# Splitting the low parts of the normalised rows between GpSimd and VectorE, ahead of a mixture-of-experts gather

## The reference

```python
xn = rms_norm(h, ffn_norm_g)                     # rows of 1024, scaled by 1/rms, times a gain
group_prob = softmax(xn @ w_rg + b_rg)           # 4 groups, the best one is taken
sel = (xn @ w_re + b_re)[the group's 8 experts]  # the best two of them, by softmax
for e in range(32):
    hid = silu(xn @ w_gate[e]) * (xn @ w_up[e])
    out = out + (hid * cw[..., e:e+1]) @ w_down[e]
```

## Time and profile before

| | |
|---|---|
| median of 3 runs | 946.12 us (946.02 to 948.24) |
| the profiled execution | 947.29 us |
| its span, first to last instruction | 945.3 us |
| TensorE busy | 932.9 us, 99% |
| VectorE busy | 532.9 us, 56% |
| ScalarE busy | 469.9 us, 50% |
| GpSimd busy | 4.4 us, 13 instructions |
| granted TensorE clock, mean | 0.997 of full speed |

### The profile page before, as it was taken

How to read it: one execution, slowest core, us unless ns; L and a number is a source line. 1 busy time by engine, 2 the same in 40 slices (tenths; PEclk the granted TensorE clock), 3 DMA queues, 4 the chain that set the end, 5 groups by cost and what they waited for, 6 DMA issues and landing times.

```text
span 945.3 us, 14062 instructions
## 1 busy us (share of the span) xinstructions
PE 932.9 (99%) x5793; PEld 759.7 (80%) x5793; DVE 532.9 (56%) x835; ACT 469.9 (50%) x728; POOL 4.4 (0%) x13
## 2 busy tenths in 40 slices
PE   9999999999999999999999999999999999999996
PEld 8989887888889999999889888889876565666553
DVE  5888996775766555655686875676454212122213
ACT  5588846857454544444566756445452131313113
POOL 1000000000000000000000000000000000000000
PEclk9999999999999999999999999999999999999998
DMA  9945565525555555554645735466758999999993
GB/s 322 315 138 176 180 223 178 164 104 179 178 187 191 179 179 179 178 184 152 210 152 180 231 130 164 148 244 245 272 187 321 406 409 408 409 409 409 409 409 123
DMA packets 89861, 223.55 MB, mean 236 GB/s; under 512 B 9161, under 2 KB 14018, under 8 KB 89794
## 3 DMA queue, kind: packets, MB, share of 16 engines
q1 hardware_dynamic: 87488, 219.62, 64.8%
q10 hardware_dynamic: 2306, 2.99, 0.9%
HBM read 221.54 MB, written 1.05 MB: 235 GB/s over the span
## 4 chain that ended last, share of the span: by engine, by line
PE 95%; DMA 3%; DVE 1%; ACT 0%; issue 0%; ACTq 0%
PE pb L494 22%; PE pb L496 21%; PE pb L495 21%; PE pb L2505 11%; PE pb L2528 5%; PE pb L2545 3%; DMA my<-in_w_exp_down 2%; PE pb L2479 2%; PE pb L584 2%; PE pb L664 1%; PE pb L652 1%; PE pb L751 1%; PE pb L635 1%; PE pb L602 1%; PE pb L728 1%; PE pb L558 1%
## 5 line engine op out<-in xcount | busy, mean ns | idle before, releaser
L1567 DVE TENSOR_TENSOR wl<-raw,wh 128x2048 fp32r<-128x2048 f32 (+3 forms) x112 | 246.3, 2207 | 96.3 <-ACT wh L1017 96.0
L1017 ACT ACTIVATE wh<-raw 128x2048 fp32r<-128x2048 f32 (+3 forms) x112 | 206.7, 1853 | 110.3 <-PE pb L496 102.3
L494 PE MATMUL pb<-wh,th 128*128 128x512 f32 (+2 forms) x620 | 245.8, 396 | 0.0
L496 PE MATMUL pb<-wh,tl 128*128 128x512 f32 (+2 forms) x620 | 239.0, 385 | 0.0
L495 PE MATMUL pb<-wl,th 128*128 128x512 f32 (+2 forms) x620 | 238.6, 385 | 0.0
L494 PE MATMUL pb<-th,wh 128*128 128x256 f32 x528 | 152.7, 289 | 0.0
L495 PE MATMUL pb<-tl,wh 128*128 128x256 f32 x528 | 149.3, 283 | 0.0
L496 PE MATMUL pb<-th,wl 128*128 128x256 f32 x528 | 149.3, 283 | 0.0
L496 PEld LDWEIGHTS pb<-wh,tl 128*128 128x128 f32 x620 | 116.4, 188 | 23.3
L494 PEld LDWEIGHTS pb<-wh,th 128*128 128x128 f32 x620 | 116.5, 188 | 23.0 <-issue 2.2
L495 PEld LDWEIGHTS pb<-wl,th 128*128 128x128 f32 x620 | 116.7, 188 | 20.7
(11 more groups left out here) (424 smaller groups left out, 1116.8 us busy)
## 6 DMA issues: line engine op xcount, KB each, us to landing
raw<-in_w_in SPq DMA_DIRECT2D x31, 1024.0 KB, 5.5
raw<-in_w_up SPq DMA_DIRECT2D x16, 1024.0 KB, 5.6
raw<-in_w_down SPq DMA_DIRECT2D x16, 1024.0 KB, 6.1
raw<-in_w_exp_up SPq DMA_DIRECT2D x10, 1024.0 KB, 15.7
raw<-in_w_xkv SPq DMA_DIRECT2D x8, 1024.0 KB, 5.1
raw<-in_w_exp_down SPq DMA_DIRECT2D x8, 1024.0 KB, 17.5
raw<-in_w_exp_gate SPq DMA_DIRECT2D x6, 1024.0 KB, 18.2
S<-in_w_exp_down SPq DMA_DIRECT2D x6, 1024.0 KB, 17.1
```

The source lines that it names most:

```text
L494: PE.matmul(o, lh, rh, start=start, stop=False, skip_group_check=True)
L496: return PE.matmul(o, ll, rh, start=False, stop=stop, skip_group_check=True)
L1017: ACTE.activation(hi_of(i), raw_of(i), ACT.Copy).then_inc(S["hi"], 1)
L1567: DVE.tensor_tensor(lo_of(i), raw_of(i), hi_of(i).bitcast(F), ALU.subtract).then_inc(S["lo"], 1)
```

## The change

The low parts of the first token tile are no longer made by VectorE but by GpSimd, in two instructions of 128x1024: the view of `X` times the root into a new tile `XT0`, and `XT0` minus the high part into XNL. GpSimd waits for the root (`rs`) before the first, and for ScalarE's first high half (`xn_hi`) before the second. VectorE makes the four low parts of the second tile. TensorE's low pairs wait for both.

```diff
@@ pool_main
             POOL.memset(SEL0[:, :].bitcast(F).rearrange("p (a n) -> p a n", n=64)[:, :, CAP:64], 0.0).then_inc(S["zero"], 1)
+            hi, lo = [x[:, 0] for x in XN4]
+            POOL.wait_ge(S["used"], ROUTER + 1)
+            POOL.wait_ge(*scaled("ffn"))
+            POOL.tensor_scalar(XT0, by_chunks[:, 0], rs_of["ffn"][:, 0:1], None, ALU.mult).then_inc(S["xn_scaled"], 1)
+            POOL.wait_ge(S["xn_hi"], 1)
+            POOL.wait_ge(S["xn_scaled"], 1)
+            POOL.tensor_tensor(lo, XT0, hi.bitcast(F), ALU.subtract).then_inc(S["xn_lo0"], 1)
@@ dve_route
             for r in range(4):
-                for t in range(2):
-                    low(t, r)
+                low(1, r)
@@ pe_gather
                 if q == 0 and 1 in parts:
-                    PE.wait_ge(S["xn_lo"], 2 + 2 * (k // 2))
+                    PE.wait_ge(S["xn_lo0"], 1)
+                    PE.wait_ge(S["xn_lo"], 1 + k // 2)
@@ build
         XN = [sbe("XNH", 2048, R, normed), sbe("XNL", 2048, R, normed)]
+        XT0 = sbe("XT0", 1024, F, normed)[:, :].rearrange("p (k q) -> p k q", k=8)
```

More of the change, by code:

```diff
@@ L153 @@
      "t2_mm", "t2", "xs_mm", "xmax", "xexp", "xprob", "xt_mm", "xt", "xv_mm", "xo_hi", "xo_lo", "xs_scaled", "logits",
-     "route_e", "mask_d", "xo_first", "rank_mm", "root", "sums", "flag", "rank", "weights", "xn_hi", "xn_lo",
+     "route_e", "mask_d", "xo_first", "rank_mm", "root", "sums", "flag", "rank", "weights", "xn_hi", "xn_lo", "xn_scaled", "xn_lo0",
      "sel", "cs_w", "ch_mm", "ch", "g_mm", "g_x", "rise_t", "rise_g", "ht_mm", "ht", "half_mm", "yy_hi", "yy_lo", "spread",
```

## The result

Over eight executions each, the kernel before took 946.77 us in the median (946.02 to 948.24), the changed one 949.12 (948.44 to 951.30). The ratio is 1.0025, with a 95% interval of 1.0016 to 1.0034: 2.4 us slower, 1.5 to 3.2. A second series, with other executions of both, gave 1.0023 (1.0013 to 1.0032). That is clear of zero, and both ratios lie within 0.3%, "same" by the bound of the prediction, though their intervals reach just past it. The profiled execution took 949.51 us with a span of 948.0, 2.7 us more than before.

What follows compares the result with a forecast made beforehand. The chain before SyncE's issue at 722.75 us was taken to bound the kernel, passing on one for one to the end; +3.59 holding - 1.29 gain = +2.3, 948.4 us against the median 946.12, range 944.8 to 951.0.

Steps and rivals of the forecast that it cites:

- Step 1: TensorE's gather: with VectorE making four of eight low parts, it takes 4.69 instead of 5.98 us, a gain of 1.29.
- Step 2: GpSimd's strided 128x1024 scaling, starting at 703.2 us once the root is known: takes 2.56 us, bounds 0.9 and 5.1.
- Step 3: GpSimd's contiguous 128x1024 subtraction after ScalarE's first high half: 2.56 us, ending 709.7, before TensorE asks; by itself free.
- Step 4: Routing chain: VectorE steps with two SBUF inputs wait until GpSimd's reading instruction is over, delaying the chain 3.59 us.
- rival two: Routing chain: scaling slow or late, so holding lasts longer; +3.9 us (950.0) to +5.2 (951.3); chance 0.13.
- Step 5: GpSimd's library reload, moved to after the memset at 699.66 us: 3.1 us of cover, costed at nothing.
- clock rival: TensorE, held idle 3.6 us before the gather, drops to half clock: +7.0 us at most, 953.1; chance 0.05.

Runs made afterwards that it cites:

- contiguous variant: The changed kernel with only GpSimd's scaling, reading X in memory order, result unused, and VectorE making all eight low parts: 948.44 us, one execution.
- the memsets: The changed kernel with six GpSimd memsets of XT0 during the routing instead of its arithmetic, VectorE making all low parts: 948.04 us, one execution.
- the subtraction alone: The changed kernel without GpSimd's scaling; GpSimd subtracts the high half from itself, result unused, and VectorE makes all eight low parts: 948.67 us, one execution.
- the version with the early copy: GpSimd only copies the first token tile of X into chunk order ahead of the root; VectorE makes all eight low parts: ratio 0.9984 to the kernel before.
- the halves: The changed kernel with only GpSimd's scaling, cut into two 128x512 instructions, results unused, VectorE making all low parts: 948.32 us, one execution.
- three fillers: The kernel before with three instead of nine filler matmuls (results unread) ahead of the rank matmuls, GpSimd idle: ratio 1.0007 to the kernel before.

## Why the prediction was right, and where it was not

The forecast was +2.3 us (948.4 against a median of 946.12), the result +2.4. Its bounding argument held: what is lost before 722.7 us arrives at the end. Its mechanism, VectorE steps with two SBUF inputs held by GpSimd, was at work. But that the number came so close was luck: it came out by errors that cancel, and one of the rivals happened too.

- *Step 1, the gain, 1.29 us.* Measured 0.85. The failed step is "the same 32 for the next expert set, which wait for nothing, take 4.69 us". The first set's gather is another one: undisturbed by low parts it still takes 5.06. Its chunks 6 and 7 wait for ScalarE's copies, which I had checked against the expert matmuls only; that is 0.20 us of the difference, and the rest stays open.
- *Step 2, the scaling, 2.56 us.* Measured 3.85, inside its bounds of 0.9 and 5.1. The contiguous variant took 2.85, so the steps of eight cost 1 us on GpSimd.
- *Step 3, the subtraction, 2.56 us.* Measured 2.39, from 707.11 (forecast 707.13).
- *Step 4, the holding, 3.59 us.* Measured 2.53. For the subtraction it was right: a two-input step waits until GpSimd has ended. Its price was put too high, 2.29 us where it cost 1.78: a two-input step was just under way when GpSimd began, and a reduction followed it, so VectorE made use of 0.5 us of GpSimd's 2.4. For the scaling, "such a step waits until the GpSimd instruction is over" was wrong: the held step ended 2.2 us after the start and cost 0.74 us; held to its end, the scaling of 3.85 us would have cost about 2.5. The Trainium skill, "SBUF — State Buffer", section "SBUF: two separate sides", has the lock kept for the whole instruction; the subtraction's rows agree, the scaling's do not, and the measurement decides. Its exemption of GpSimd instructions that only write agrees with the memsets. The longer GpSimd part, which was rival two's condition, came true without its consequence.
- *Step 5, the reload.* Nothing, as costed: the first arithmetic behind it took 1.89 us with the subtraction alone. In the version with the early copy the reload was issued at 700.6, and the copy started at 700.71 and took 3.82 us, no more than the scaling elsewhere. The 6 us that the Trainium skill's "GPSIMD Engine Reference", section "Instruction dispatch", gives for a first call after a load did not appear in any run.
- *The clock rival, at 0.05.* It happened in both profiled executions of the change. The one row I had read, a clock that falls 4.1 us after the last matmul, made 3.6 us look nearly safe. The step that failed is taking that delay as the length of idleness that is needed: in the change the clock fell 4.1 us after the fillers' end too (707.55 to about 711.7), but TensorE had been at work again from 710.24 on, and that did not stop it. (Nor is the delay always 4.1: it was 5.0 in the second profile of the change, 3.2 in the subtraction alone and in the halves, 2.5 with three fillers.) In these runs it fell after waits of 1.1 to 2.75 us. Its price was 1.3 us, of at most 4.7.

In sum: 2.53 for the held steps, 1.34 for the clock, less 0.86 for the gain (5.91 - 5.05) makes 3.0 by the rows, where the forecast had 3.59 + 0 - 1.29 = 2.3. The hold was put 1.06 us too high, the clock's 1.34 us were left out, and the gain was put 0.43 us too high; 0.7 us did not cancel, and the rows' 3.0 is still within the interval of the measured 2.4 (1.5 to 3.2).

## What to carry to other kernels

GpSimd is no free second engine beside VectorE: what it read from SBUF in the middle of this chain of two-input VectorE steps lengthened the chain by 0.74 us (one input) and 1.7 us (two inputs), so ask which steps run beside it, and give it the part that can be done before the chain begins. A wait opened ahead of TensorE can have two prices, the wait and matmuls behind it at half clock (1.3 us here); fillers must be sized again when a chain grows. And when a gather is freed from one producer, look for the next one in its own order of banks and copies, not in a neighbouring gather's pace.

## What the runs showed that I had not expected

- A one-input GpSimd instruction holds VectorE for a part of its length only: 2.2 of 3.85 us (128x1024, steps of eight), 1.3 of 2.07 (128x512, steps of eight), at most 1.22 of 2.85 (128x1024, contiguous).
- TensorE's clock fell after waits of 1.12 us (the halves), 1.87 (the subtraction alone) and 2.69 to 2.75, and not after 0.91 or 0.16, one profiled execution for each but the change's two. Where the limit lies, and whether it is always the same, they do not show.
- Reading in steps of eight elements costs VectorE 0.26 us for each 128x256 low part (0.74 against 0.48), as much as the steps cost ScalarE for as many elements (2.14 against 1.07 us for 128x1024).
